# Placing the small expert-phase tiles 64 bytes apart instead of 256 bytes in the on-chip memory

## The reference

```python
def swiglu(h, wg, wu, wd):                     # wg, wu: 1024 x 2816; wd: 2816 x 1024
    return (silu(h @ wg) * (h @ wu)) @ wd

def moe(h, router, wg, wu, wd):                # layer 1
    vals, idx = lax.top_k(h @ router, 2)
    gates = softmax(vals)
    comb = sum(one_hot(idx, 8) * gates[..., None], axis=-2)
    out = zeros_like(h)
    for e in range(8):
        out = out + comb[..., e:e+1] * swiglu(h, wg[e], wu[e], wd[e])
    return out
```

## Time and profile before

| what | value |
|---|---|
| median of three runs | 1358.5 us |
| the profiled execution's own time | 1358.0 us |
| its span, first to last instruction | 1356.2 us |
| TensorE matmuls busy | 1276.2 us (94%) |
| VectorE busy | 943.9 us (70%) |
| ScalarE busy | 804.8 us (59%) |
| GpSimd busy | 146.1 us (11%) |
| mean granted TensorE clock, share of full | 0.964 |

### The profile page before, as it was taken

The page is one execution under the profiler, slowest core; times in us unless marked ns, Lnnn a source line. Parts: engine busy times, 40 slices in busy tenths (PEclk is TensorE's granted clock), DMA queues, the critical chain, the costliest instruction groups (busy, mean ns, idle before and its releaser), DMA issues.

```text
span 1356.2 us, 18493 instructions
## 1 busy us (share of the span) xinstructions
PE 1276.2 (94%) x6873; PEld 1044.6 (77%) x6873; DVE 943.9 (70%) x918; ACT 804.8 (59%) x797; POOL 146.1 (11%) x132
## 2 busy tenths in 40 slices
PE   5978989999989999699999999999999999999993
PEld 3447579999975567488888888888888888888882
DVE  2656345444335656378898898898888988988983
ACT  2446343343224554267787777867867877778773
POOL 2011000000000010100030120210300401201301
PEclk9978989999989989699999999999999999999997
DMA  8241084454150531779999999999999999999995
GB/s 303 58 112 32 10 269 156 157 178 148 48 183 0 115 98 40 263 281 341 359 394 370 369 402 368 365 404 355 382 387 373 383 377 380 385 375 353 410 356 188
DMA packets 125836, 356.96 MB, mean 263 GB/s; under 512 B 8848, under 2 KB 34160, under 8 KB 125760
## 3 DMA queue, kind: packets, MB, share of 16 engines
q1 hardware_dynamic: 121248, 342.34, 69.4%
q0 software_dynamic: 4144, 12.82, 3.3%
q10 hardware_dynamic: 400, 1.20, 0.2%
HBM read 348.04 MB, written 9.48 MB: 264 GB/s over the span
## 4 chain that ended last, share of the span: by engine, by line
PE 86%; issue 6%; DVE 3%; ACT 2%; DMA 1%; POOL 1%; SPq 0%; POOLq 0%; DVEq 0%; ACTq 0%
PE ps L1906 33%; PE ps L1926 15%; PE ps L1824 11%; PE ps L1620 8%; PE ps L1840 5%; PE ps L1730 1%; PE ps L1777 1%; PE ps L1914 1%; PE ps L1683 1%; PE ps L1561 1%; PE ps L1675 1%; PE ps L1695 1%; PE ps L1607 1%; PE ps L1785 1%; PE ps L1745 1%
## 5 line engine op out<-in xcount | busy, mean ns | idle before, releaser
L1130 DVE TENSOR_TENSOR w_lo<-ring,w_hi 128x2048 fp32r<-128x2048 f32 (+1 forms) x326 | 684.7, 2126 | 184.8 <-ACT w_hi L824 181.1
L824 ACT ACTIVATE w_hi<-ring 128x2048 fp32r<-128x2048 f32 (+1 forms) x326 | 574.6, 1783 | 224.4 <-PE ps L1926 69.5
L1906 PE MATMUL ps<-w_hi,xg_hi 128*128 128x512 f32 (+1 forms) x768 | 288.5, 376 | 2.5 <-DVE xg_lo L1499 2.5
L1906 PE MATMUL ps<-w_hi,xg_lo 128*128 128x512 f32 (+1 forms) x768 | 286.7, 373 | 0.0
L1906 PE MATMUL ps<-w_lo,xg_hi 128*128 128x512 f32 (+1 forms) x768 | 286.0, 372 | 0.0
L1906 PEld LDWEIGHTS ps<-w_hi,xg_hi 128*128 128x128 f32 x768 | 145.1, 189 | 28.6 <-issue 2.9
L1906 PEld LDWEIGHTS ps<-w_lo,xg_hi 128*128 128x128 f32 x768 | 144.6, 188 | 25.9
L1906 PEld LDWEIGHTS ps<-w_hi,xg_lo 128*128 128x128 f32 x768 | 145.0, 189 | 24.9
L1926 PE MATMUL ps<-w_hi,am_hi 128*128 128x512 f32 x352 | 138.5, 393 | 0.0
L1926 PE MATMUL ps<-w_lo,am_hi 128*128 128x512 f32 x352 | 137.2, 390 | 0.0
L1926 PE MATMUL ps<-w_hi,am_lo 128*128 128x512 f32 x352 | 137.0, 389 | 0.0
(11 more groups left out here) (278 smaller groups left out, 1408.2 us busy)
## 6 DMA issues: line engine op xcount, KB each, us to landing
ring<-in_moe_w_down SPq DMA_DIRECT2D x80, 1024.0 KB, 7.8
ring<-in_moe_w_gate SPq DMA_DIRECT2D x68, 1024.0 KB, 9.2
ring<-in_moe_w_up SPq DMA_DIRECT2D x66, 1024.0 KB, 9.6
ring<-in_moe_w_gate SPq DMA_DIRECT2D x32, 768.0 KB, 7.0
ring<-in_moe_w_up SPq DMA_DIRECT2D x32, 768.0 KB
ring<-in_ffn_w_gate SPq DMA_DIRECT2D x11, 1024.0 KB
ring<-in_ffn_w_up SPq DMA_DIRECT2D x11, 1024.0 KB, 5.1
ring<-in_ffn_w_down SPq DMA_DIRECT2D x10, 1024.0 KB, 4.9
```

The source lines that it names most:

```text
L824: A(hi[:, 0:size], src[:, 0:size], ACT.Copy).then_inc(hi_ready, 1)
L1130: V.tensor_tensor(lo[:, 0:size], src[:, 0:size], hi[:, 0:size].bitcast(F32), ALU.subtract).then_inc(lo_ready, 1)
L1906: ins = mm_(ps[:, b + c0 // 512, 0:c1 - c0], (xg_hi, xg_lo)[xp][:, k, :], w[wp][:, k % 2, c0:c1], start=(k == 0 and n == 0), stop=(k == KD ...
```

## The change

```diff
         class Carve:
-            def __init__(self, start, line=16):
-                self.at, self.line = start, line
+            def __init__(self, start):
+                self.at = start

             def __call__(self, name, *shape, dt=F32):
                 n = 1
                 for s in shape:
                     n *= s
-                start, self.at = self.at, self.at + (n + self.line - 1) // self.line * self.line
+                start, self.at = self.at, self.at + (n + 15) // 16 * 16
                 return at(name, start, [P, *shape], dt)
 ...
-        carve = Carve(PHASE + 2 * SLOT_W * MOE_PAIRS, 64)
+        carve = Carve(PHASE + 2 * SLOT_W * MOE_PAIRS)
```

## The result

The changed kernel takes 1363.7 us in the median of eight, against 1358.4 us for the kernel before; these two medians lie 5.3 us apart. The ratio estimated from the repeated runs is 1.0051 with a 95% interval of 1.0039 to 1.0062, which is 5.3 to 8.4 us, about 7 us slower, where no change was forecast. The profiled execution took 1364.2 us with a span of 1362.4 us.

The account below looks back on a forecast made before the run. TensorE's own pace was taken to bound the expert loop, without gaps. All terms were 0 except 0.1 us for two transfers, so 1358.5 + 0.1 = 1358.6 us, with an 8-in-10 range of 1357.1 to 1360.6 us.

Parts of the forecast that it names:

- (a): Down products' 1056 stationary loads from am_hi and am_lo: moved addresses cost 0, protected by 38.7 ns of cover.
- R2: Slower: am_hi and am_lo loads outgrow their cover, losing 2.7 us at 229.3 ns or 14.0 at 240; chance 0.03.
- R3: Faster: tiles at the same rest conflict; moving them saves down products up to 14.2 us, giving 1344.4 us; chance 0.04.
- R1: Slower: GpSimd writes two descriptors per row in indirect transfers, 4.7 us on the path, giving 1363.2 us; chance 0.03.
- (c) and (d): First fetch into xr and last addition from y_out, 512 KB each, on the path: 0.1 us together, ends -1.4 and +2.8.
- The terms for VectorE, ScalarE and GpSimd: Work of these engines on moved tiles: 0 us, since idle time and cover keep any growth from TensorE.

Follow-up runs that it names:

- am_even: Changed kernel with only am_hi and am_lo put back to multiples of 256 bytes; 1357.2 us in the median of twelve, ratio 0.9991.
- all_odd: Kernel before with w_hi, w_lo, am_hi, am_lo, xg_hi, xg_lo all 64 bytes past a multiple of 256; timed again as all_odd_timed, ratio 0.9999.
- am_odd: Kernel before with only am_hi and am_lo moved 64 bytes on; 1363.8 us in the median of five, ratio 1.0050.
- am128_xg64: Kernel before with am_hi, am_lo at rest 128 and xg_hi, xg_lo at rest 64 (address modulo 256); loop 775.27 us, no launch ratio.
- w_odd: Kernel before with only the weight tiles w_hi and w_lo moved to rest 64; expert products stepped at 228.9 ns, no launch ratio.
- cols112_odd: Kernel before with am at rest 64 and down products taking 112 of 128 stationary columns; down products stepped at 226.7 ns.

## Why the prediction was wrong

**The step that failed is (a),** the load of the down products' stationary operand, which I took as 0. It measured 7.0 us. Two things in that step were wrong. It reasoned from the recorded length of a load, 188 ns, against a step of 226.7 ns, and called the 38.7 ns between them cover. The load did stay at 188 ns, and the step from matmul to matmul still grew by 16 cycles. The time beside another operation was taken to be free, and here it wasn't. And the step knew of the 13.4 ns beside the 512 columns, and filed them as "something else". That was the term that could move: 13.4 ns above the estimated 213.3 at distance 0, 20.0 ns at 64.

**Rival R2** had the right place, the 1056 loads, and the wrong mechanism: it wanted loads longer than the cover. With the condition "loads above 227 ns" it would have been called refuted by the trace of after, in which the loads are 188 ns and the loss is there all the same. It was given 0.03.

**Rival R3** had the right kind of mechanism, a conflict that depends on how the operands lie to each other, with the wrong sign. It took the place at which all tiles have the same rest for the bad one; for these products it is the best of eight. The argument used against it, that both products have the same pace though their tiles lie at quite different distances from the weights, failed because modulo 256 they all had distance 0. The witness in the earlier trace rows, `xg` beside `am`, was no witness for an odd distance, as the step itself said, and 0 was taken nevertheless.

**R1** didn't come: the additions are still issued in 3.65 to 3.69 us, with 125836 packets as before. That its 1363.2 us lie near the measured time is chance. **Terms (c) and (d)** were right in being small. That 0.1 us was forecast for the pair and -0.01 and 0.14 us were measured is luck, since the last addition takes 7.94 us in am_even with `y_out` at rest 64 and 8.37 us in all_odd_timed with `y_out` at rest 0: it scatters by more than the term. The terms for VectorE, ScalarE and GpSimd were right too; am_even shows them together as no difference.

The Trainium skill, in "SBUF — State Buffer", section "A bandwidth-pool intuition that's wrong (but worth ruling out)", gives TensorE a second and independent read port for the loads. By that a load's place would not matter to the matmul beside it. In timing the traces of am_odd and all_odd don't agree: with the same 188 ns of load the matmuls step at 233.3 or 226.7 ns by its place relative to the moving operand. Whether a port is where the two meet, no run here shows.

**What is shown and what is not.** Shown: the loss comes from the place of the down products' stationary tiles (am_odd alone makes it to 0.6 us, am_even alone removes it), it goes with the distance between stationary and moving operand and not with either rest (all_odd), and `xg` pays as `am` does, save in the third chunk (am128_xg64). That the distance counts modulo 256 rests on the kernel before as well: by the addresses `xg_hi` lies 36 and `am_hi` 299 steps of 256 bytes from the first `w_hi`, one even and one odd, and both products step at 226.7 ns. Argued only: that the two reads get in each other's way in the on-chip memory. Two groups that don't pay fit this without proving it. The transposes of `act_m` moved from distance 128 to 192 (their moving operand, the identity in `cst`, begins at rest 128) and eight of them take 1.03 us both times. The float32 products of line 1620 start 0.43 us apart for 512 columns, nearly twice the time for the same bytes, whether the slice of `hT` begins at rest 0 or 128. Open: why 128 and 192 cost less than their neighbours, why the first expert of w_odd and the groups of 60 in cols112_even step slower than their fellows, why 112 columns exchange the good distance for the bad one, and why the third chunk and the dense products follow another order.

## What to carry to other kernels

When a change only moves tiles, ask of each matmul that is the bound how its stationary and moving operand lie to each other, and read the distance between starts, not the lengths of loads or matmuls. Here 128 stationary float32 columns beside 512 moving ones ran best with both at the same address modulo 256, wherever that was; rounding all big tiles to 256 bytes gets this for free, and it has to be measured again for another length of either operand, as the third chunk and the dense products show. An engine at 100% busy has no cover: every ns that its instructions can grow is on the path.

## What the runs showed of the hardware

- Matmuls of 512 columns, each with its own load of 128 stationary columns, stepped at 226.7 to 234.3 ns at 2.4 GHz by the distance between the two operands' addresses modulo 256, with the recorded length of the loads at 187 to 189 ns in the mean throughout. The load is hidden in full beside a matmul by the profile, and its place still shows in the pace.
- The same distance, 192 bytes, gave 233.3 ns in parts of the first expert and 229 ns in the seven later ones of the same run (w_odd).
- 112 or 64 stationary columns in place of 128 made the products slower at distance 0 (229.0 and 230.0 ns in the groups of 48, against 226.7 ns).
- 512 KB into or out of tiles at rest 64 in place of 0 made no difference that shows: first gather 4.28 and 4.35 us at rest 64, 4.19 to 4.32 at rest 0; last addition 8.16 and 7.94 us at rest 64, 8.01 to 8.37 at rest 0.
- The stretch ahead of the expert loop scatters by 5.4 us (first product at 572.6 to 578.0 us) between executions, though only w_odd and all_odd move tiles of the dense phase. An effect of a few us is read from the loop's own length, or needs many runs.
